# The recurrent layer of a diffusion trunk: gate order reversed, output panels begun in the last scan, low weight parts made by GpSimd

## What is computed

```
def rglru_scan(x, w_gate, b_gate, lam, h0):
    xb = x.reshape(b, s, LRU_BLOCKS, LRU_BLK)
    g = jnp.einsum('bsnk,gnkj->gbsnj', xb, w_gate).reshape(2, b, s, D_RNN)
    g = g.astype(jnp.float32) + b_gate.astype(jnp.float32)[:, None, None, :]
    r, i = jax.nn.sigmoid(g[0]), jax.nn.sigmoid(g[1])
    log_a = -LRU_C * r * jax.nn.softplus(-lam.astype(jnp.float32))
    a = jnp.exp(log_a)
    u = jnp.sqrt(-jnp.expm1(2.0 * log_a)) * (i * x.astype(jnp.float32))
...
    _, hs = lax.associative_scan(_linear_combine, (a, u), axis=1)
    return hs

def lru_mixer(h, w_in, conv_w, conv_b, w_gate, b_gate, lam, w_out, ctx):
    gate_branch, xr = jnp.split(h @ w_in, 2, axis=-1)
    xr = centred_conv(xr, conv_w, conv_b)
...
    hf = rglru_scan(xr, w_gate[0], b_gate[0], lam[0], h0f)
    hb = jnp.flip(rglru_scan(jnp.flip(xr, axis=1), w_gate[1], b_gate[1], lam[1], h0b), axis=1)
    y = (hf + hb).astype(h.dtype) * jax.nn.gelu(gate_branch)
    return y @ w_out, (state,)
```

## Time and profile before

| | |
|---|---|
| median of 3 runs | 3441.18 us (3436.58 to 3443.45) |
| profiled execution | 3440.55 us, its span 3438.8 us |
| TensorE's mean granted clock | 0.98 |
| ScalarE busy | 1121.0 us (33%) |
| GpSimd busy | 64.8 us (2%), all in the first 400 us |
| six looped turns of the recurrent layer | 2743.5 to 2867.8 us |
| turns 6 and 7 | 2867.8 to 2905.4 us |
| output projection behind them | to about 2960 us |

### The profile page before, as it was taken

The page is one execution under the profiler, slowest core; times in us unless marked ns, Lnnn a source line. Parts: engine busy times, 40 slices in busy tenths (PEclk is TensorE's granted clock), DMA queues, the critical chain, the costliest instruction groups (busy, mean ns, idle before and its releaser), DMA issues.

```text
span 3438.8 us, 53095 instructions
## 1 busy us (share of the span) xinstructions
PE 3277.2 (95%) x20608; PEld 3026.2 (88%) x20608; DVE 2004.5 (58%) x3058; ACT 1121.0 (33%) x1801; POOL 64.8 (2%) x48
## 2 busy tenths in 40 slices
PE   7899999999999998999999988999999987999999
PEld 4777689999997775999999866899999887999999
DVE  3333357777576665666863755666763888633333
ACT  3244433111145554421112444321111586311111
POOL 1211000000000000000000000000000000000000
PEclk9999999999999999999999999999999998999999
DMA  5111124455221110244532200244532221222222
GB/s 192 55 53 41 40 64 135 157 175 167 68 81 38 44 43 17 68 159 150 174 99 67 74 19 19 61 159 142 171 110 69 72 61 49 74 73 73 73 73 79
DMA packets 436801, 304.27 MB, mean 88 GB/s; under 512 B 12483, under 2 KB 414534, under 8 KB 435654
## 3 DMA queue, kind: packets, MB, share of 16 engines
q1 hardware_dynamic: 426340, 293.75, 28.3%
q10 hardware_dynamic: 10338, 8.88, 0.8%
HBM read 298.49 MB, written 4.10 MB: 88 GB/s over the span
## 4 chain that ended last, share of the span: by engine, by line
PE 85%; DVE 7%; ACT 3%; issue 1%; DVEq 1%; DMA 0%; ACTq 0%; SPq 0%
PE psB L351 29%; PE psA L351 29%; PE psD L351 7%; PE psC L414 3%; PE psA L395 3%; PE psC L367 2%; PE psB L395 2%; PE psC L406 2%; DVE work L2339 1%; PE psB L952 1%; PE psD L893 1%; PE psA L952 1%; DVE act_lo L2347 1%; DVE work L2664 1%; PE psD L925 1%
## 5 line engine op out<-in xcount | busy, mean ns | idle before, releaser
L1633 ACT ACTIVATE w_hi<-raw 128x1024 fp32r<-128x1024 f32 (+1 forms) x315 | 325.8, 1035 | 1092.1 <-PE psB L351 733.9
L2230 DVE TENSOR_TENSOR w_lo<-raw,w_hi 128x1024 fp32r<-128x1024 f32 (+1 forms) x315 | 376.0, 1195 | 312.1 <-ACT w_hi L1633 311.9
L351 PE MATMUL psA<-act_hi,w_hi 128*128 128x320 f32 x1536 | 355.0, 312 | 15.6 <-DVE w_lo L2230 14.9
L351 PE MATMUL psA<-act_hi,w_lo 128*128 128x320 f32 x1536 | 355.7, 313 | 0.0
L351 PE MATMUL psB<-act_hi,w_lo 128*128 128x320 f32 x1536 | 354.5, 312 | 0.0
L351 PE MATMUL psA<-act_lo,w_hi 128*128 128x320 f32 x1536 | 352.5, 311 | 0.0
L351 PE MATMUL psB<-act_hi,w_hi 128*128 128x320 f32 x1536 | 351.4, 310 | 0.0
L351 PE MATMUL psB<-act_lo,w_hi 128*128 128x320 f32 x1536 | 351.1, 310 | 0.0
L2260 DVE SCALAR_TENSOR_TENSOR work<-work,silu_c 128x1024 f32<-128x1024 f32 x266 | 330.0, 1282 | 12.6 <-issue 0.4
L351 PEld LDWEIGHTS psA<-act_hi,w_hi 128*128 128x128 f32 x1536 | 261.3, 190 | 17.6 <-issue 16.7
L351 PEld LDWEIGHTS psB<-act_hi,w_hi 128*128 128x128 f32 x1536 | 260.7, 189 | 0.0
(11 more groups left out here) (359 smaller groups left out, 5616.9 us busy)
## 6 DMA issues: line engine op xcount, KB each, us to landing
raw<-in_w_ffn_in SPq DMA_DIRECT2D x176, 512.0 KB, 3.8
work<-in_w_mod SPq DMA_DIRECT2D x152, 512.0 KB, 4.2
raw<-in_w_ffn_out SPq DMA_DIRECT2D x64, 512.0 KB, 4.1
raw<-in_w_ffn_out SPq DMA_DIRECT2D x32, 384.0 KB, 3.4
raw<-in_diff_w_in SPq DMA_DIRECT2D x24, 512.0 KB, 3.8
work<-in_w_mod SPq DMA_DIRECT2D x8, 1024.0 KB, 7.0
raw<-in_lru_w_in SPq DMA_DIRECT2D x16, 512.0 KB, 4.2
raw<-in_w_mod SPq DMA_DIRECT2D x12, 512.0 KB, 4.1
```

The costliest lines, as they stand in the source:

```text
L351: last = nc.tensor.matmul(out[:, b, 0:half], w[slot][:, kt * cols + c0:kt * cols + c0 + P], r[:, o:o + half], start=(kt == 0 and p == 0), ...
L1633: nc.scalar.activation(w_hi[s][:, 0:n], raw[s][:, 0:n], ACT.Copy).then_inc(hi_done, 1)
L2230: nc.vector.tensor_tensor(w_lo[s_][:, 0:n], raw[s_][:, 0:n], w_hi[s_][:, 0:n].bitcast(F32), ALU.subtract).then_inc(split_done, 1)
```

## The change

Five things, all in layer 3:
1. gates(i) runs rb (psD), if (psC), rf (psB) and then the fourth (psA); ScalarE's tanhs follow in that order. Only rf waits for "gelu" now.
2. The low parts of xr panels 2 to 7, gate panels 2 to 7 and of wg 1 to 7 are made by GpSimd (lru_low_parts), in the same order on the slots' semaphores.
3. The high part of wo3 panel 0 is made by ScalarE at the end of turn 6, its low part by VectorE behind "o" of turn 6.
4. Panel 1's high and low parts are both made by VectorE in turn 7 behind L2680.
5. project for wo3 runs the first two panels in a pair: kt 0 to 6 of panel 0, kt 0 to 6 of panel 1, then the wait for "o" of turn 7, then kt 7 of both.

```
-        LRU_PE = Steps(sem("lru_pe"), ["rf", "if", "rb"], 1)
+        LRU_PE = Steps(sem("lru_pe"), ["rb", "if", "rf"], 1)
...
+            def lru_low_parts(i, left):
+
+                for kind, ahead in (("xr", 2), ("wg", 1), ("gate", 2)):
+                    if left < ahead:
+                        continue
+                    s_, n = LRU_SLOT[kind], (4 if kind == "wg" else KT) * P
+                    pool.wait_ge(hi_done, lru_at(kind, i, phases["lru"].dense_first + 1, ahead))
+                    nc.gpsimd.tensor_tensor(w_lo[s_][:, 0:n], raw[s_][:, 0:n], w_hi[s_][:, 0:n].bitcast(F32),
+                                            ALU.subtract).then_inc(split_done, 1)
...
+            pool.wait_ge(split_done, lru_at("gate", 1, phases["lru"].first + 1))
+            with pool.Fori(0, KT - 2) as i:
+                lru_low_parts(i, 2)
+            lru_low_parts(KT - 2, 1)
...
+                if paired:
+                    for part in (range(kts - 1), range(kts - 1, kts)):
+                        if part[0]:
+                            last_source()
+                        for j in range(2):
+                            if not part[0]:
+                                pe.wait_ge(split_done, phases[name].number(0, j))
+                            last = products(pe, psum[j], phases[name].slots[j], kts, P, 0, *rows, 0, T, TH, part)
+                            if part[0]:
+                                last.then_inc(gemm_done, 1)
+                turns_and_mods(turn, 1 if paired else 0, KT // 2, plan, place)
...
-                        for g, ps, name in ((0, psB, "rf"), (1, psC, "if"), (2, psD, "rb"), (3, psA, None)):
+                        for g, ps, name in ((2, psD, "rb"), (1, psC, "if"), (0, psB, "rf"), (3, psA, None)):
...
-                        else:
-                            for j in range(2):
-                                high_part("wo3", 0, j)
                         LRU_DVE.wait(act, "m", i)
                         LRU_ACT.mark(nc.scalar.activation(l_th2, l_th2, ACT.Sqrt), "sq")
                         if left > 0:
                             gelu_branch(i, 1)
                         if left > 1:
                             lru_high("gate", i, 2, lru_at("gate", i, ph.first + 1, 1))
+                        elif left:
+                            high_part("wo3", 0, 0)
...
-                        if left > 1:
-                            lru_low("xr", i, 2)
                         LRU_ACT.wait(dve, "t", i)
...
+                        else:
+                            wo = phases["wo3"]
+                            dve.wait_ge(raw_in[1], 16 * (wo.landed[1] + 1))
+                            dve.wait_ge(gemm_done, wo.first)
+                            nc.vector.tensor_copy(w_hi[1][:, 0:KT * P], raw[1][:, 0:KT * P]).then_inc(hi_done, 1)
+                            low_part("wo3", 0, 1)
                         LRU_ACT.wait(dve, "a2", i)
                         LRU_DVE.mark(nc.vector.scalar_tensor_tensor(l_th2, l_tr2, 0.25, l_th2, ALU.add, ALU.mult), "m")
-                        if left > 0:
-                            lru_low("wg", i, 1)
-                        else:
-                            first_low_parts(3)
...
-                        if left > 1:
-                            lru_low("gate", i, 2)
+                        if left == 1:
+                            dve.wait_ge(split_done, phases["wo3"].first)
+                            low_part("wo3", 0, 0)
```

More of the change, by code:

```diff
@@ L974, in _, with project @@
             x_tiles = [KT]
-            def project(name, kts, rows, last_source, plan=None, place=None):
+            def project(name, kts, rows, last_source, plan=None, place=None, paired=False):
                 base = x_tiles[0]
@@ L987, in turn @@
                                  before_last=last_source if j == 0 else None).then_inc(gemm_done, 1)
-                turns_and_mods(turn, 0, KT // 2, plan, place)
+                if paired:
[9 more added lines that the diff above has]
+                turns_and_mods(turn, 1 if paired else 0, KT // 2, plan, place)
                 x_tiles[0] += KT
@@ L1479, in _ @@
                     LRU_DVE.wait(pe, "o", KT - 2)
-                project(f"wo{layer}", KT, (act_hi, act_lo), lambda: mixed.wait_turns(pe, KT))
+                project(f"wo{layer}", KT, (act_hi, act_lo), lambda: mixed.wait_turns(pe, KT), paired=layer == 3)
                 ph = phases[f"in{layer}.0"]
@@ L2029, in lru_block @@
                             lru_high("xr", i, 2, lru_at("xr", i, ph.first + 1, 1))
-                        for g, ps, dst, ready, read in ((0, psB, l_tr[0], "rf", "trf"), (1, psC, l_ti[0], "if", None),
-                                                        (2, psD, l_tr[1], "rb", None), (3, psA, l_ti[1], None, "t")):
+                        for g, ps, dst, ready, read in ((2, psD, l_tr[1], "rb", None), (1, psC, l_ti[0], "if", None),
+                                                        (0, psB, l_tr[0], "rf", "trf"), (3, psA, l_ti[1], None, "t")):
                             if g == 1:
```

## The result

| | median | runs, lowest to highest | profiled execution (its span) |
|---|---|---|---|
| before | 3439.04 us | 11 runs, 3435.74 to 3443.45 | 3440.55 us (3438.8) |
| changed | 3453.35 us | 11 runs, 3448.07 to 3462.08 | 3461.31 us (3459.5) |

The ratio is 1.004, with the interval 1.003 to 1.005: 14.3 us slower by the medians. The forecast was 3450 us, in a range of 3440 to 3460, and 8.9 us slower than before.

The account below looks back on a forecast made before the run. VectorE's queue was taken to bound the recurrent layer's loop. Loop +14.2 (-12.5 + 23.7 + 3.0), scans' end -3.8 and early panels -1.5 gave +8.9 us on 3441.18, thus 3450 us, range 3440 to 3460.

Parts of the forecast that it names:

- the second rival: Loop's 512-column parts all cost 1.0 us; TensorE's longer half clock at output panels 1 to 3: +11.9, 3453, chance 0.25.
- Low parts taken from VectorE: In the loop, VectorE saves five pairs of 1024-column low parts at 2.27 us and gate 7 at 1.13: -12.5 us.
- Eleven large parts on GpSimd: In the loop, each 1024-column low part on GpSimd stalls VectorE by 2.15 us: 23.7 us.
- Six parts of 512 columns: In turns 1 to 6, each stalls VectorE 0 to 1.0 us by who goes first; half taken, 3.0 us.
- (a) The end of the scans: Last turn: tanhs no longer wait for the gelu, so L2691 starts at 2893.2 instead of 2897.05: -3.8 us.
- (b) The early panels: Output projection: 84 matmuls run before act's last tile, but the third panel waits for its low part: -1.5 us.
- The first (small parts free): In the loop, the 512-column parts cost nothing as L504 and L2685 go first: +5.9, 3447, chance 0.2.
- The third (no stall of long instructions): In the loop, GpSimd's reads don't hold up long VectorE instructions: -17.8, 3423, chance 0.12.
- The fourth: Last turn: panel 1's copy and low part come after a2, giving back half of 5.3: +11.5, 3452, chance 0.05.
- the forecast's own branch: The main case, with half cost for the 512-column parts: +8.9 us, 3450 us, chance 0.38.
- The signs: New profile: VectorE instructions stretched 1 to 2.4 us, turns about 23 us, TensorE waiting before psB and the third panel.
- The sign called wrong: Counting against the forecast: GpSimd instructions over 2.4 us because it waits, or unchanged VectorE durations and 18.6 us turns.

Follow-up runs that it names:

- The experiment with the unused tile: Changed kernel with all low parts back on VectorE, GpSimd subtracting in a tile the layer doesn't use at the same three places each turn: 3460.05 us.
- the first experiment: Changed kernel with the low parts back on VectorE, gate order and early panels kept: 3436.44 us, ratio 0.999 to before.
- the third experiment: Changed kernel with only the 512-column low parts (wg) back on VectorE: 3450.01 us, ratio 1.0023 to before.
- the one with writes: Changed kernel with all low parts back on VectorE, GpSimd filling unused columns at the same places behind a one-column subtraction: 3442.32 us, one run.
- The last experiment: Kernel of the first experiment, with VectorE's low part directly behind the addition into x in layer 3's output projection: 3433.77 us, ratio 0.9977 to before.

## Why the prediction was right, and where its sum was off

Its mechanism stands. The undisturbed part of the sum and the stall were read rightly, two terms were mis-sized in the same direction, and the time came out 3 us above the forecast, at the second rival's 3453. The change came out further off than the time: +14.3 us by the medians where +8.9 was forecast. The forecast had started from a median of three runs, 3441.18, and the eleven runs have 3439.04; that these 2.1 us made up for a part of the error is luck.

**Low parts taken from VectorE, -12.5 us.** Held: the turn's account above closes with 2.27 for a pair.

**Eleven large parts on GpSimd, 11 x 2.15.** Held: 2.18 and 2.05 in the trace. The rows that it came from the earlier trace rows were of 16-column instructions of layer 0, and the step to scans of 512 columns was the boldest of the prediction. The experiment with the unused tile shows it by itself. By the Trainium skill (SBUF — State Buffer, "Who interferes with whom") a reading GpSimd instruction blocks a two-input VectorE one for its whole length; the trace agrees, the scans included, with 1.67 to 2.18 us of stall against 1.89 and 2.40 of GpSimd.

**Six parts of 512 columns, 6 x 0.5 = 3.0 us.** This term was mis-sized. It had left open who goes first, and took half of 1.0. They cost 1.11 in turns 1 to 5 each, 5.5 in all, and nothing in turn 6. The timelines show why. (A part "asks" where its row starts.) In the turn shown above GpSimd asks at 2780.99, in the middle of L504, 0.22 us ahead of L2713's start at 2781.21. It waits for L504's end (1.46 us, where half of the 2.40 of a 1024-column part would be 1.2) and then goes ahead of L2713. In turn 6 the order is the other way round by 0.06 us, VectorE's row and GpSimd's:

```profile
2898.41 1.49 DVE L2713 SCALAR_TENSOR_TENSOR work<-work 128x1288 f32<-128x1288 f32 x1
```

```profile
2898.47 2.57 POOL L858 TENSOR_TENSOR w_lo<-raw,w_hi 128x512 fp32r<-128x512 f32 x1 [12.11 <-ACT w_hi L2039]
```

Now VectorE is undisturbed and GpSimd waits. TensorE in turn waits 4.4 us for that low part, at no cost to what follows: from turn 6's start to the last "u" it is 25.40 us, and 25.43 in the first experiment, which hasn't got that wait. The forecast had the request 0.1 us behind L504's start. It came 0.53 behind (2780.46 and 2780.99), as ScalarE's L2071 started 0.26 us behind the end of L2732 (2772.57) and not right at it, but still during L504, and so it won in all five turns. Such a meeting is worth one side or the other, and not half of it; which one has to be settled turn by turn. Here it was the same in turns 1 to 5, but that is no rule of loops: in the third experiment the scan won in two turns and GpSimd in three, and in the one with writes the cast took 1.05, 2.15, 1.06, 2.15 and 0.49 us in turns 0 to 4. The one side also makes the loop +16.4 where +14.2 was forecast: 11 x 2.1 + 5.5 - 12.5 = 16.1.

**(a) The end of the scans, -3.8 us.** Measured -3.9. The gate order gives 2.0 us of the gain by itself.

**(b) The early panels, -1.5 us.** Mis-sized, with the wrong sign: +0.6. What was forecast of the wait came true: TensorE restarts on the third panel 6.7 us behind act_lo (2925.58 to 2932.28; forecast 6.6), with a wait of 4.5 where "about 4" was named. From the windows above the panel takes 9.61 us at a clock of 0.77. TensorE's rows:

```profile
2932.28 0.90 PE L351 MATMUL psA<-act_hi,w_hi 128*128 128x320 f32 x2 [4.54 <-DVE w_lo L2254]
2932.97 0.73 PE L351 MATMUL psA<-act_lo,w_hi 128*128 128x320 f32 x2
...
2936.70 0.49 PE L351 MATMUL psA<-act_hi,w_lo 128*128 128x320 f32 x2
2937.04 0.46 PE L351 MATMUL psA<-act_hi,w_hi 128*128 128x320 f32 x2
```

Before, TensorE came to the same panel without a pause, and it took 7.19 us at the clock 1.00:

```profile
2913.90:2921.09 7.19, 7.19 (x50) 7.19 (x49) 4.84 (x9) 2.15 (x4) 0.00 (x0) 1.00 0.29 86
```

The wait was priced and what the clock does behind it was not: the first matmuls take 0.73 us a pair, at the 1.2 GHz level, and only behind 2936.7 0.46, at 2.4 GHz. The panel takes 2.4 us longer by that, a little more than the term's error of 2.1. In the six traces with a wait of 4.5 to 4.6 us the panel takes from 9.05 to 10.08 us. The last experiment confirms it: with a wait of 1.85 us the panel keeps the clock 1.00, and the gain that the early panels were made for comes in. In the forecast's second rival a late TensorE was named, as 1 to 3 us at the start of the panels; it came two panels later.

**The sum:** forecast +14.2 - 3.8 - 1.5 = +8.9, measured +16.4 - 3.9 + 0.6 = +13.1 in the layer. The medians have +14.3, with an interval of the ratio that goes from 10 to 17 us.

**The rivals.** The first (small parts free) falls with the third experiment, since they cost 5.5. The third (no stall of long instructions) falls with every trace. The fourth falls: L2713 of turn 7 follows the second low part at 2914.39, after waiting 0.31 us for ScalarE's L2077, so panel 1 was ready in time. The second, in which all small parts cost their full length and TensorE loses by the clock, is what happened, save for turn 6. It had a chance of 0.25, the forecast's own branch 0.38.

**The signs.** The stretched instructions, the waits for a tanh, the matmuls inside the last scan and the new wait are all there. The turn is 23.95 us where about 23 was named, and L2713 of turn 7 stands 8.5 us behind the end of turn 6's scans instead of 10.5, 2.0 earlier where 1.5 was named. The sign called wrong, a part of GpSimd longer than 2.4 us because it is the one that waits, showed in turn 6 only (2.57).

What is open: why GpSimd's subtraction takes 1.89 us with the same columns of one tile as both inputs and 2.40 with two tiles. Its product of a tile with one repeated column takes 1.89, too. No kernel was run on it.

## What to carry to other kernels

An elementwise step that reads SBUF and is moved from VectorE to GpSimd isn't free when VectorE sets the loop's time and mostly reads two SBUF tiles: it cost this loop nearly GpSimd's duration, 2.1 us for each step that VectorE had done in 1.13. Look first at what stands under a wait already; the 0.69 us low part under the square root cost nothing on VectorE and 1.1 us on GpSimd in five turns of seven. And when work is begun early, find the step that is waited for next and put it first in its engine's queue: without that order the early matmuls brought nothing, with it 4.1 us. Then look at what was put behind: 1.0 us of it was lost again in the next norm.

## What the runs showed of the hardware

- A GpSimd subtraction in SBUF held a VectorE instruction with two SBUF inputs that began just behind it, scans included, for its own duration less about 0.2 us (2.05 to 2.18 for 2.40, 1.67 and 1.72 for 1.89). Copies of one column beside it took their usual 0.15 us.
- A GpSimd instruction that only writes (a fill of 128x2048, 1.81 us) leaves scans, products and subtractions with two inputs alone, but held a cast of 640 columns for up to 1.66 us (2.15 instead of 0.49).
- Of two that meet, the one that asked first goes first, down to 0.02 us (2779.94 and 2779.96 in the third experiment). One that asks during the other's instruction waits for its end and then comes ahead of what stands behind it, even where VectorE's instructions stand end to end.
- A wait of 4.5 to 4.6 us of TensorE was followed by 3 to 6 us at 1.2 GHz (the panel at a granted clock of 0.73 to 0.82 in six traces), one of 1.85 us by none (1.00).
